# Ten transformer sublayers on one core: a chunk's wait split, the last norm rearranged, the condition rows spread on the chip, the first modulation formed in columns

## The reference

```
SUBS = ["mla", "ffn", "fourier", "ffn", "ffn", "mix", "ffn", "ffn", "mix", "ffn"]
```

```python
def ada(cvec, w, b):
    return jnp.split(jax.nn.silu(cvec) @ w + b, 6, axis=-1)
# first sublayer: both conditions meet the same weights
sh1, sc1, g1, sh2, sc2, g2 = [m[:, None, :] for m in ada(c, ada_w[i], ada_b[i])]
csh1, csc1, cg1, csh2, csc2, cg2 = ada(c_ctx, ada_w[i], ada_b[i])
h_l = rmsnorm(x, norm1_g[i]) * (1 + sc1) + sh1
...
# end of the last sublayer
y = swiglu_2(modulate(x, mod, 2), ffn_w_in[l, 1], ffn_w_out[l, 1])
x = layer_norm(DN_ALPHA * x + 0.5 * sub_gate(mod, 2) * y, ln_g[l, 2], ln_b[l, 2])

def layer_norm(x, g, b):
    mu = jnp.mean(x32, axis=-1, keepdims=True)
    var = jnp.mean(jnp.square(x32 - mu), axis=-1, keepdims=True)
    return (x32 - mu) * lax.rsqrt(var + LN_EPS) * g + b
```

## Time and profile before

| | |
|---|---|
| median of three runs | 2124.78 us (2124.2 to 2128.8) |
| the profiled execution's own time | 2124.72 us |
| its span | 2122.9 us |
| TensorE busy | 2084.2 us (98%) |
| VectorE busy | 1272.6 us (60%) |
| ScalarE, GpSimd busy | 422.6 us (20%), 495.0 us (23%) |
| mean granted TensorE clock | 0.991 |
| read from HBM | 434.20 MB, 206 GB/s over the span |

### The profile page before, as it was taken

How to read it: one execution, slowest core, us unless ns; L and a number is a source line. 1 busy time by engine, 2 the same in 40 slices (tenths; PEclk the granted TensorE clock), 3 DMA queues, 4 the chain that set the end, 5 groups by cost and what they waited for, 6 DMA issues and landing times.

```text
span 2122.9 us, 24027 instructions
## 1 busy us (share of the span) xinstructions
PE 2084.2 (98%) x9428; PEld 1675.1 (79%) x9428; DVE 1272.6 (60%) x2509; ACT 422.6 (20%) x804; POOL 495.0 (23%) x411
## 2 busy tenths in 40 slices
PE   7999999999999999999999999999999999999997
PEld 4777888688876887687788888688868868888865
DVE  5546588746776466746523687777776653346554
ACT  3334211022110111033130311031102323122101
POOL 0100244402543244300000144414440000002340
PEclk9999999999999999999999999999999999999998
DMA  9673576775768564842334475766574333444431
GB/s 376 248 268 98 201 285 244 275 264 204 298 241 297 200 245 188 293 166 103 155 124 154 160 281 236 273 235 242 227 256 174 131 154 119 159 158 159 153 134 70
DMA packets 61551, 437.85 MB, mean 206 GB/s; under 512 B 6976, under 2 KB 8768, under 8 KB 40448
## 3 DMA queue, kind: packets, MB, share of 16 engines
q1 hardware_dynamic: 28608, 317.82, 38.8%
q0 software_dynamic: 32256, 117.45, 15.8%
q10 hardware_dynamic: 576, 1.05, 0.1%
HBM read 434.20 MB, written 2.10 MB: 206 GB/s over the span
## 4 chain that ended last, share of the span: by engine, by line
PE 88%; DVE 7%; DMA 2%; POOL 1%; issue 1%; ACT 1%; SPq 1%; ACTq 0%; DVEq 0%; POOLq 0%
PE lin L1881 27%; PE small_ps L2027 18%; PE lin L2027 13%; PE small_ps L2089 5%; PE lin L2122 5%; PE lin L2089 4%; PE small_ps L1881 3%; PE lin L2353 3%; PE pstat L2004 1%; PE lin L2278 1%; DVE proj L1131 1%; DVE ada_ring L1095 1%; PE small_ps L2372 1%; DMA ada_ring<-in_ada 1%; DMA rec<-in_ada_pe 1%
## 5 line engine op out<-in xcount | busy, mean ns | idle before, releaser
L1881 PE MATMUL lin<-h,ring 128*128 128x256 f32 x1968 | 434.2, 382 | 4.4 <-ACT h L1000 2.4
L1881 PEld LDWEIGHTS lin<-h,ring 128*128 128x128 f32 x1968 | 373.9, 191 | 60.1 <-issue 8.8
L630 POOL TENSOR_TENSOR proj<-ring 128x1024 f32<-128x1024 f32 x54 | 127.8, 2366 | 836.6 <-DVE xc L1310 633.4
L1095 DVE CUSTOM_DVE_ANT_0 ada_ring<-ada_ring,crow 128x1024 f32<-128x1024 f32 x224 | 265.9, 1220 | 32.9 <-DMA ada_ring<-in_ada 32.5
L615 POOL DMA_DIRECT2D ada_ring<-in_ada x224 | 121.4, 542 | 702.3 <-DVE sums L1095 667.8
L2027 PE MATMUL small_ps<-ring,h 128*128 128x256 f32 x864 | 195.6, 379 | 4.8 <-DVE sq L1112 4.8
L2027 PEld LDWEIGHTS small_ps<-ring,h 128*128 128x128 f32 x864 | 163.8, 190 | 28.4 <-issue 6.2
L2027 PE MATMUL lin<-proj,sq 128*128 128x256 f32 x672 | 153.9, 379 | 0.0
L2027 PEld LDWEIGHTS lin<-proj,sq 128*128 128x128 f32 x672 | 127.7, 190 | 17.4
L1881 PE MATMUL lin<-rec,ring 128*128 128x258 f32 (+2 forms) x608 | 139.5, 380 | 0.0
L1881 PEld LDWEIGHTS lin<-rec,ring 128*128 128x128 f32 x608 | 115.2, 190 | 16.8
(11 more groups left out here) (428 smaller groups left out, 3038.0 us busy)
## 6 DMA issues: line engine op xcount, KB each, us to landing
ring<-in_w SPq DMA_DIRECT2D x66, 2048.0 KB, 8.9
ada_ring<-in_ada POOLq DMA_DIRECT2D x224, 512.0 KB, 5.9
ring<-in_w2a SPq DMA_DIRECT2D x30, 1536.0 KB, 7.7
ring<-in_gates SPq DMA_DIRECT2D x12, 2048.0 KB, 8.0
ring<-in_w2d SPq DMA_DIRECT2D x12, 1408.0 KB, 7.3
ring<-in_mproj SPq DMA_DIRECT2D x8, 2048.0 KB, 7.9
ring<-in_mtok SPq DMA_DIRECT2D x4, 2048.0 KB, 8.2
ring<-in_branch SPq DMA_DIRECT2D x4, 2048.0 KB, 7.6
```

What stands on the lines that cost most here:

```text
L630: W(combined_weights(j, 0), b12, b11, ALU.subtract).then_inc(s_weights_combined, 1)
L1095: V.tensor_tensor_reduce(w, w, crow[:, 0 if s < FIRST2 else 1], 1.0, 0.0, ALU.mult, ALU.add, sums[:, s % 3, b:b + 1]).then_inc(s_ada_used, 1)
L1881: ins = mm(dst, w[:, lo:lo + m], rhs(k), start=k == 0, stop=k == nk - 1)
```

## The change

Four edits that are independent of each other:

1. **Chunk's wait split.** TensorE's wait for all four sums of `h` moves from before product 1 to before product 3 of the first chunk, and in folded sublayers product 5 waits for the last `raw_scaled` in place of the unit that is taken one step later.
2. **Condition rows.** The two conditions are loaded as one row of 4 KB each in place of 512 KB each; TensorE spreads them to 128 partitions by four matmuls of a 1x128 row of ones with 512 columns, and ScalarE's Silu reads the result from PSUM in four halves. `bias_rows_made` uses the same banks and so moves behind the first two blocks.
3. **Columns.** `first_modulation` has the weights as stationary operand (128x128) and the two condition columns moving, so its results are columns at once; `first_turned` and ScalarE's copies go. The last two blocks are loaded in halves in the order 6a, 7a, 6b, 7b, and `in_a`'s weights in halves too. The squares of the first norm are added on VectorE to two tiles, so TensorE has two matmuls there in place of eight. `tables_and_bounds` and the context's modulation move behind the scaling of `x`.
4. **Last norm.** Halfway through the last result tile TensorE sums the other seven; VectorE centres these by a seventh of their mean and adds their squares (`final_first_tiles`) ahead of taking the last tile. Afterwards one matmul gives the mean of all, one the sum of squares, the mean's square is taken off for the variance (`final_norm`), and VectorE scales the last two tiles in place of ScalarE.

```diff
@@ gate_and_up
                 h_tile(KD - 1)
-                pe.wait_ge(s_h_combined, 4 * (f + 1))
                 for j in range(CHUNKS):
...
                     if j:
                         turn_hidden(s, j - 1)
+                    else:
+                        pe.wait_ge(s_h_combined, 4 * (f + 1))
                     part(3, combined_h(3), b22)
                     if j:
                         pe.wait_ge(s_second_gate, before + j)
+                    elif folded(s):
+                        pe.wait_ge(s_raw_scaled, RAW * raw_before(s) + RAW)
                     else:
                         pe.wait_ge(*taken(u0 + RAW - 1))
@@ SP queue
-            for dst, src in ((sil[0:BUCKETS], I["onehot"]), (work[0:BUCKETS], I["relb"])):
-                sp.dma_start(dst, src).then_inc(s_bucket_tables_dma, 16)
+            sp.dma_start(condition_rows[0], I["crow"][0:1, 0]).then_inc(s_crow_dma, 16)
+            sp.dma_start(condition_rows[1], I["crow_ctx"][0:1]).then_inc(s_crow_dma, 16)
             sp.dma_start(cols[:], I["cols"]).then_inc(s_cols_dma, 16)
-            sp.dma_start(crow[:, 0], I["crow"][:, 0]).then_inc(s_crow_dma, 16)
-            sp.dma_start(ctx_row, I["crow_ctx"]).then_inc(s_crow_dma, 16)
...
+                if n < FIRST_N - 2:
+                    sp.dma_start(first_weights(n), src).then_inc(s_ada_first_dma[n], 16)
+                else:
+                    for last in (FIRST_N - 2, FIRST_N - 1):
+                        first_half(last, n + 2 - FIRST_N)
+                if n == 1:
+                    for dst, src in ((sil[0:BUCKETS], I["onehot"]), (work[0:BUCKETS], I["relb"])):
+                        sp.dma_start(dst, src).then_inc(s_bucket_tables_dma, 16)
@@ ScalarE
-            A(crow[:, 0], crow[:, 0], ACT.Silu)
-            A(ctx_row, ctx_row, ACT.Silu).then_inc(s_silu_rows, 1)
+            for i, row in enumerate((crow[:, 0], ctx_row)):
+                for half in range(2):
+                    act.wait_ge(s_row_spread, nth(act, s_row_spread))
+                    A(row[:, half * 512:half * 512 + 512], pa[2 * i + half][:], ACT.Silu).then_inc(s_silu_rows, 1)
...
@@ TensorE, first_modulation
-                    for k in range(KD):
-                        ins = mm(lin[i // 2][0:2, i % 2 * T:i % 2 * T + T], csil[:, 0:2, k],
-                                 first_weights(n)[:, k * T:(k + 1) * T], start=k == 0, stop=k == KD - 1)
...
+                    for m in range(2):
...
+                        for k in range(KD):
+                            ins = mm(lin[2][:, 4 * i + 2 * m:4 * i + 2 * m + 2], first_weights(n)[:, m * D + k * P:m * D + (k + 1) * P],
+                                     csil[:, 0:2, k], start=k == 0, stop=k == KD - 1)
@@ results
+                        if s + 1 == len(subs) and m == KD - 1 and k == KF // 2:
+                            pe.wait_ge(s_tiles_added, nth(pe, s_tiles_added, KD - 2))
+                            mm(pa[2][:, 0:T], ones[:], rstd[:], start=True, stop=True).then_inc(s_mean_sums, 1)
@@ TensorE, order
+            def condition_spread():
+
+                pe.wait_ge(s_crow_dma, nth(pe, s_crow_dma, 2))
+                for i in range(2):
+                    for half in range(2):
+                        mm(pa[2 * i + half][:], ones[0:1], condition_rows[i][:, half * 512:half * 512 + 512],
+                           start=True, stop=True).then_inc(s_row_spread, 1)
...
-                    bias_rows_made()
+                    condition_spread()
                     pe.wait_ge(s_silu_c, nth(pe, s_silu_c))
                     first_modulation(BY_PE[0:2])
-                    squares_summed()
-                    first_modulation(BY_PE[2:4])
+                    bias_rows_made()
+                    pe.wait_ge(s_first_squares_added, 1)
...
+                    first_modulation(BY_PE[2:4]).then_inc(s_first_sums, 1)
...
-            mean_summed()
-            folded_squares_summed()
+            for n, done in enumerate((s_final_mean, s_final_squares)):
+                pe.wait_ge(s_final_parts, n + 1)
+                mm((pstat, pa[3])[n][:, 0:T], ones[:], yab[:, n], start=True, stop=True).then_inc(done, 1)
```

More of the change, by code:

```diff
@@ L253, in build @@
         s_bucket_tables_dma = sem("bucket_tables_dma")
+        s_row_spread = sem("condition_row_spread")
+        s_ada_first_half_dma = [sem(f"first_half_of_last_first_ada_weights{i}") for i in range(2)]
+        s_first_latents_dma = sem("first_latents_weights_dma")
+        s_first_squares_added = sem("first_squares_added")
         s_tiles_added = sem("tiles_added")
@@ L419, in spectral, with raw_before @@
             return s < len(subs) and subs[s] == "fourier"
+        def raw_before(s):
+            return sum(folded(n) for n in range(s))
         def folds_before(s):
@@ L987, in _ @@
                     squares(sq, x, before if s else None)
+                    if s == 0:
+                        bias_rows_out()
                     deviation()
-                if kind == "mla":
-                    for i in range(2):
-                        act.wait_ge(s_first_rows, nth(act, s_first_rows))
-                        A(first_rows(i), lin[i][0:2], ACT.Copy).then_inc(s_first_rows_taken, 1)
                 if not folded(s) and not spectral(s):
@@ L1786, in _ @@
                 if kind == "mla":
+                    tables_and_bounds()
+                    context_modulation()
                     ada(ADA_BEFORE_CONTEXT)
```

164 lines of the change are left out of this document (123 added, 41 removed).

## The result

The changed kernel takes 2141.2 us (median of 6 runs, 2139.86 to 2141.84) against 2125.72 for the kernel before in the same session (6 runs): a ratio of 1.0067, 95% interval 1.0055 to 1.0079. It is slower, by 15.5 us of medians, and lies 8.7 us above the upper end of the predicted range. The profiled execution took 2139.86 us (span 2138.1), 15.2 more in span than the one before.

What follows compares the result with a forecast made beforehand. TensorE, busy 2084.2 of 2122.9 us, was taken as the bound, with time to win only where it idles or runs slowly. Head +9.5, chunks -2.3, tail -2.9 gave +4.3 on 2124.72: 2129.1 us, range 2124.0 to 2132.5.

Steps and rivals of the forecast that it cites:

- The head, +9.5: Program start up to `h`: clock stays at 1.2 GHz, column blocks take 6.8 us, `h` at 48.6 against 39.17.
- The rival in which the clock rises: Head: busy TensorE is granted 2.4 GHz by about 15 us, `h` at 37.0, total 2117.5 us; chance 0.10.
- Behind `h`, 0 with 1.7 either way: First projections after `h`: slow-clock stretches may move by an unknown amount, so 0 with 1.7 us either way.
- The chunks, -2.3: Three gaps at the first chunks of sublayers 6, 7, 9: gains 0.1, 0.65, 1.5 us; bounds -0.8 and -4.8.
- Sublayer 9's 1.5: First chunk of sublayer 9: with no modulation products there, the split wait gains 1.5 us.
- the forecast's +4.3: Whole kernel: sum of head, chunks and tail, 9.5 - 2.3 - 2.9, on the profiled execution's 2124.72 us.
- The end, -2.9: Last norm: reciprocal starts 2.6 us earlier, stores win 0.5, slow matmuls cost 0.2; bounds -1.8 and -3.9.
- its 1.2: Last norm: the last result tile is taken 1.2 us later than 2104.46, as VectorE is free at 2105.7.
- The check marks: Signs expected in the new profile, such as 6.8 us blocks, `h` near 48.6, reciprocal 7.2 after TensorE's last tile sum.
- the mark on L1243: Sublayer 6: the second chunk's first matmul would wait for L1243, the adding of `first_gate`.
- the small gains fail as well: Whole kernel: chunks give 0.8, tail 1.8, clock comes back 1.7 later; +8.6, 2133.3 us; chance 0.10.

Runs made afterwards that it cites:

- e5: Head edits alone on the kernel before, but modulation results made as rows and turned, as before; 2123.21 us against 2126.42, ratio 0.9987.
- e6: Kernel before with the first modulation results made in columns, nothing else of the head; 2135.05 us against 2126.42, ratio 1.0033.
- e3: Kernel before with the rearranged last norm alone, including the middle matmul; 2122.94 us against 2127.29, ratio 0.9975.
- e1: Kernel before with the split wait for `combine_h` alone; 2133.79 us against 2127.29, ratio 1.0031.

## Why the prediction was wrong, point by point

**The head, +9.5: right** in mechanism and size. Spread 7.3 us, blocks 6.8 to 7.0, bias rows 7.2, `h` at 48.41 for 48.6; +9.2 in the trace. That the clock stays at 1.2 GHz until `h` was read from 32-row and 32-column matmuls and carried over to two columns, which no row had; e5 and e6 confirm it from both sides. The rival in which the clock rises fell. The Trainium skill ("TensorE: Matmul & The Clock Gate", Part 1) speaks for that rival, since it asks for no more than back-to-back matmuls; the trace disagrees, with matmuls from 2.76 to 46.4, hardly a gap between them, and the clock still down at 48.5.

**Behind `h`, 0 with 1.7 either way: +0.5** up to 104 us. The clock came back 1.2 better and stayed down 1.7 longer at 82.7. Not in the sum at all were +1.2, +1.7 and +0.7 further on (692, 953 and 1622 us), 3.6 in all, where the change touches nothing.

**The chunks, -2.3: the step that failed.** They cost +5.1 in the trace (+4.1, +2.7, -1.7), 7.4 us more than forecast, and +6.5 alone by medians. Sublayer 9's 1.5 came (1.7). In sublayer 7 the prediction let GpSimd's sum meet "VectorE's last sum of hidden units" and be held "for the sum's end", 2.36 us, as the like row in sublayer 6 took 2.45. It was the third sum, and it was held to the end of both of GpSimd's, 5.20. In sublayer 6 it argued that GpSimd's sums "start behind the third modulation load", which "doesn't move": true, they start 0.24 us behind the third sum now and 0.25 before, and the hold came all the same. The trace of before had rows for the longer price, which the prediction passed over; they stand in other sublayers and on other operations (timeline of the kernel before):

```profile
370.25 4.05 DVE L1273 COPY rec<-modc 128x8 f32<-128x8 f32 x1
370.68 1.82 POOL L648 TENSOR_TENSOR proj<-ring 128x768 f32<-128x768 f32 x1
372.45 1.81 POOL L649 TENSOR_TENSOR proj<-ring 128x768 f32<-128x768 f32 x1
...
841.37 3.93 DVE L1269 TENSOR_TENSOR modc<-modc,ada_b 128x8 f32<-128x8 f32 x1
```

A copy of 8 columns takes 4.05 us, through both of GpSimd's operations, and an addition of 8 columns 3.93 (0.17 elsewhere in the same trace); 1332.90 and 1547.18 us have two more such rows. With these the lower bound would have been a loss of about 2.6 us in sublayer 6 and 1.5 in sublayer 7 before any change of the clock (estimates: a third sum of 5.2 us from 1221.66 and from 1436.10, then 0.75 for the fourth and `first_gate`, against 1225.05 and 1440.59).

The condition needs more than these rows. In the kernel before, the third sum has the same lead and goes through:

```profile
1221.66 0.42 DVE L1142 TENSOR_TENSOR yab<-yab,big 128x256 f32<-128x256 f32 x1
1221.91 2.38 POOL L630 TENSOR_TENSOR proj<-ring 128x1024 f32<-128x1024 f32 x1
```

What differs is that there product 6, for which GpSimd's sum waits too, (the first half of 16 matmuls that run from 1219.74 to 1223.36) ended only near 1221.6, while GpSimd was issuing its modulation load; after the split it ends over a microsecond sooner against VectorE, and the sum stands ready behind that load. All 17 profiled executions bear this out. In them 74 operations of VectorE without an operand in PSUM begin while GpSimd issues such a load, 0.11 to 0.27 us after its wait for the following sum has ended and 0.25 to 0.44 ahead of that sum, and all 74 are held to the end of the second sum. Those that begin earlier are not held, among them this third sum in the seven executions without the split, where it begins 0.01 to 0.02 us before the wait's end. That an operation of GpSimd which already stands ready takes the ports earlier than its recorded start would fit; no run varies this alone, so the reason stays a guess.

**The clock behind a missed wait** wasn't priced: 1.3 and 1.2 us in the first trace, more in the second. The prediction knew a clock that falls under slow forms of matmuls; here it fell behind 4.1 and 3.0 us of standing still, while the gaps of 1.6 to 1.7 before had left it alone.

Taken together the trace came out 10.9 us above the forecast's +4.3: 7.4 in the chunks, 3.6 in the three places that were not in the sum and 0.5 behind `h`, less 0.3 in the head and 0.6 at the end, which makes 10.6.

**The end, -2.9: mechanism right, size 0.6 too small in the trace.** The forecast had the middle matmul's 0.43 in it, so -3.9 + 0.4 = -3.5 is what answers to it, and 4.35 by e3's medians. The last tile was taken 0.6 us after its sums ended where the prediction's own times make 0.8 (2105.7 against 2104.9; its 1.2 holds the middle matmul as well). The additions of squares ran as estimated (1.88 for the first three, from 0.73 + 0.73 + 0.45); from the last tile to the reciprocal it was 5.7 us for 5.9.

**The check marks** of the prediction on blocks, `h`, the wait for L1243 in sublayer 6 and no gap in 9 all came true; the mark on L1243 said a wait, and no length. The reciprocal came 6.3 us after the end of TensorE's sums and not 7.2; the prediction's own times would give 6.7 (0.8 + 5.9). The rival "the small gains fail as well" (2133.3) was the nearest and still 8 us off, because no case let an edit that removes waits cost time.

## What to carry to other kernels

When an edit lets one engine start earlier, search the trace for the longest time that any operation of its neighbours took beside it, not for the time of the nearest like one, and put that into the lower bound; VectorE's operations that read SBUF alone, beside two sums of GpSimd in a row, are the case here. Keep such operations out of the line between a PSUM bank and the engine that waits for it: moving four sums of 0.42 us behind the chunk turned +6.5 us into -4.9. And a wait of a busy TensorE costs more than its length when the clock falls in it or behind it.

## What was not expected of the hardware

An addition of 0.42 us on VectorE was held for 5.18 to 5.20 us, through two of GpSimd's in a row (2.36 and 2.34), six times in three profiled executions (the changed kernel's two and e1's), while additions with an operand in PSUM kept their 0.42 beside the same GpSimd operations. In all 17 profiled executions it was the operations that began 0.11 us and more after GpSimd's wait had ended that were held, though all began 0.25 us and more ahead of GpSimd's sum.

Column matmuls with two moving columns, TensorE busy and its weight loads back to back, not only failed to raise the clock; it fell during them, in e6 from 2.4 GHz at 35.1, 2.3 us into the block. During 32-row matmuls of 512 columns it fell in e5, at 23.0.

TensorE stood still for 1.6 us without a change of its clock, and for 3.0 and 4.1 us with one, followed by 3.2 or 6.6 us at 1.2 GHz; the same kernel showed either. Between 100 us and the last norm the 17 profiled executions have nine waits of 2.35 to 4.12 us, and the clock fell in or just behind each; the wait of 1.93 us near 700 us was followed by a fall in five of them and by none in twelve.
